# RWKV-7 inverse in 32x32 diagonal blocks, with VectorE's transpose in place of a second product chain

## The chip, the cores and the metric
The kernel runs on one core of one Trainium2 chip. The metric is the device time of one execution in microseconds (us); lower is better. Before the change it is 1394.63 us, the median of three runs (1394.05 to 1394.86).

## The reference
Two transformer-like blocks follow each other on 256 tokens of width 1024. The change touches one part of the second: the RWKV-7 state recurrence of its first layer, for 16 heads of 64:

```python
def step(S, inp):
    r_t, w_t, k_t, v_t, a_t, b_t = inp
    sa = jnp.einsum('bhvk,bhk->bhv', S, a_t)
    S = S * w_t[:, :, None, :] + sa[..., None] * b_t[:, :, None, :] + v_t[..., None] * k_t[:, :, None, :]
    y = jnp.einsum('bhvk,bhk->bhv', S, r_t)
    return S, y
```

The kernel computes it in chunks of 128 tokens. Within a chunk `sa` depends on itself through a strictly lower triangular matrix A, so the vectors u of a chunk solve (I - A) u = rhs, and the kernel needs the inverse of I - A on diagonal blocks of 64.

## The kernel before
Everything outside `Rwkv`'s core is dense products of split fp32 weights (lines 291 to 293) and is not touched. The core runs 8 units: 2 chunks of 128 tokens times 4 groups of 4 heads. Two units overlap: unit u-1 is in its second half while unit u is in its first, and the two use separate PSUM banks, so one trip of the loop (a *round*) holds the first half of one unit and the second half of the one before. There is no scheduler: the order of every engine is the order in which `pe_core`, `act_core` and `dve_core` list the steps, and semaphores hold a step until its data are there.

The steps of a unit:
- *columns* (L2722): 8 transposes by TensorE, copied out by ScalarE.
- *pairs* (L2739): 8 products of 256 columns, then VectorE multiplies each of the 4 results by a mask (L3011).
- *a_mat* (L2753): A the other way round, from which VectorE starts X (L3020); Y, X's transpose, is started from the masked pairs (L3028).
- *levels* 0 to 4: block size 1, 2, 4, 8, 16 doubles to 32, and in level 5 of 6 (n = 4) to 64. Each level is *z* (L2767, A times X), a copy by ScalarE (L2947), then *xy*: X is updated by Y and Z (L2782) and Y by Z and Y (L2786), each joined under a mask by VectorE (L3035 for X, L3042 for Y). The last level makes Y only.
- *rhs* (L2797, L2800), *u_first* (L2810), *carry* (L2818, L3050), *u_second* (L2826): the solution on the first and the second 64 tokens.
- *state* (L2836, L2837, L3060; first chunk only) and *y* (L2845 to L2851, L2961).

All of it works on 64 x 64 tiles of the array. The first and second half of the tokens sit crossed (rows of one half, columns of the other), made so by the `crossed` matrix in *columns*. A product in fp32 shows in the trace as two weight loads and two matmuls, so a *z* of 8 products is 16 matmuls there.

Of the kernel before, what the change touches and what calls it, by code (L numbers as in the profile page):

```python
# [21 lines left out]
U8 = mybir.dt.uint8  # L22
# [46 lines left out]
for _n, _w in (("ident", 128), ("cos", 64), ("sin", 64), ("causal", 384), ("invalid", 384), ("dist", 384), ("tri", 129),  # L69
               ("ends", 2), ("upper", 512), ("pair", 128), ("ident64", 64), ("crossed", 128)):  # L70
    CONSTS[_n] = (_at, _w)
    _at += _w
N_CONST = _at
LEVELS = 5
HALF = P // 2
COLUMN_TILES = (slice(0, HALF), slice(HALF, P))


def shape_constants():
# [10 lines left out]
    put("crossed", np.roll(eye, HALF, 1))  # L90
# [16 lines left out]
    turned = np.roll(strict, HALF, 1)  # L107
    put("upper", np.stack([turned, full, turned, full], 1).astype(np.float32))
    put("pair", (s // HALF == t // HALF).astype(np.float32))
    r, q = (i % HALF)[:, None], np.arange(HALF)[None, :]  # L110
    put("ident64", (r == q).astype(np.float32))
    lev = np.zeros((P, 2, LEVELS + 1, HALF), np.float32)
    for n in range(LEVELS + 1):
        b = 2 ** n
        same = r // (2 * b) == q // (2 * b)
        lev[:, 0, n], lev[:, 1, n] = same & (r // b < q // b), same & (r // b > q // b)
# [60 lines left out]
def build(nc, a, out):  # L177
    with ExitStack() as ctx:
# [25 lines left out]
        levels = sb("levels", [P, 2, LEVELS + 1, HALF], U8)  # L204
# [879 lines left out]
        class SetUp:  # L1084
# [22 lines left out]
            def sp_rest(self, sp):  # L1107

                sp.dma_start(consts[:, P:N_CONST], a["consts"][:, P:N_CONST]).then_inc(levels_loaded, 16)
                sp.dma_start(levels[:, :, :, :].rearrange("p a l s -> p (a l s)"), a["levels"]).then_inc(levels_loaded, 16)  # L1110
# [1033 lines left out]
        class TimeMix:  # L2144
# [13 lines left out]
            def __init__(self):  # L2158
# [17 lines left out]
                self.identity, self.first_x, self.first_y = sem(n + "identity"), sem(n + "first_x"), sem(n + "first_y")  # L2176
                self.z, self.z_done = [sem(f"{n}z{x}") for x in range(2)], [sem(f"{n}z_done{x}") for x in range(2)]
                self.x, self.x_done = [sem(f"{n}x{x}") for x in range(2)], [sem(f"{n}x_done{x}") for x in range(2)]
                self.inv_y, self.inv_y_done = [sem(f"{n}inv_y{x}") for x in range(2)], [sem(f"{n}inv_y_done{x}") for x in range(2)]
# [33 lines left out]
                self.x_inv = [by_head(flat(3, 0, 256)), by_head(front[:, 0:256])]  # L2213
                self.y_inv = [by_head(flat(3, 256, 256)), by_head(front[:, 256:512])]
                self.z_buf = [by_head(gain_b[1][:, 512:768]), by_head(front[:, 512:768])]
# [477 lines left out]
            def crossed(self):  # L2693

                first, second = slice(0, HALF), slice(HALF, P)
                return (first, second), (second, first)

# [12 lines left out]
            def pe_columns(self, T, u):  # L2710
# [9 lines left out]
                for j in range(2):  # L2720
                    for n, slot in enumerate((7, 4, 2, 5)):
                        mm = T.e.transpose(self.stream_banks(s)[2 + j][:, n * P:(n + 1) * P], self.pair_rows(slot, t, g, j),  # L2722
                                           const("crossed") if n == 0 else ident)
                    mm.then_inc(*T.one(self.turned))

            def pe_pairs(self, T, u):
# [3 lines left out]
                T.e.wait_ge(self.cols, 2 * (u + 1))  # L2730
                if i:
                    T.e.wait_ge(self.state_done, min(u - 1, self.GROUPS))
                for j in range(2):
                    if i and j:
                        T.e.wait_ge(self.y_done, u - 1)
                    for a in range(2):
                        for e in range(2):
                            part = slice(e * HD, (e + 1) * HD)
                            mm = T.e.matmul(self.stream_banks(s)[2 * j + e][:, 256 * a:256 * a + 256], fm[part, j, 2 + a, :],  # L2739
                                            fm[part, j, 0:2, :].rearrange("p a s -> p (a s)"), start=True, stop=True)  # L2740
                            if a:
                                mm.then_inc(*T.one(self.pairs))

            def pe_a_mat(self, T, u):
# [4 lines left out]
                for j in range(2):  # L2749
                    for at, there in self.crossed():  # L2750
                        for e in range(2):
                            part = slice(e * HD, (e + 1) * HD)
                            mm = T.e.matmul(acc[at, s, e * 512 + j * HALF:e * 512 + (j + 1) * HALF], fm[part, j, 0, there], fm[part, j, 2, at],  # L2753
# [3 lines left out]
            def pe_z(self, T, u, n):  # L2757

                s, i, t, g = self.place(u)
                if n == 0:  # L2760
                    T.e.wait_ge(self.masked, 4 * u + 4)
                    T.e.wait_ge(self.first_x, 2 * (u + 1))
                else:
                    T.e.wait_ge(self.x_done[s], (LEVELS - 1) * i + n)
                for m in range(4):
                    for at, there in self.crossed():
# [3 lines left out]
            def pe_xy(self, T, u, n):  # L2770

                s, i, t, g = self.place(u)
                if n == 0:
                    T.e.wait_ge(self.first_y, 2 * (u + 1))
                else:
                    T.e.wait_ge(self.inv_y_done[s], LEVELS * i + n)
                T.e.wait_ge(self.z_done[s], LEVELS * i + n + 1)
                for m in range(4):
                    at_m = slice(m * HALF, (m + 1) * HALF)
                    if n < LEVELS - 1:  # L2780
                        for at, there in self.crossed():
                            mm = T.e.matmul(acc[at, s, 512:1024][:, at_m], self.y_inv[s][there, m, :], self.z_buf[s][there, m, :], start=True, stop=True)  # L2782
                        if m == 3:
# [1128 lines left out]
```

## Time and profile before

| | |
|---|---|
| time, median of 3 runs | 1394.63 us |
| profiled execution: span from the first to the last instruction | 1392.2 us |
| TensorE busy | 1362.8 us (98%) |
| VectorE, ScalarE busy | 855.2 us (61%), 696.6 us (50%) |
| RWKV core, from its first columns to the last unit's y | about 778 to 916 us of the span |
| one round of the core | 14.35 us |

Of the profiled execution itself only the span is given; the median of the runs lies 2.4 us above it. A busy TensorE in this profile is not TensorE at its peak: each matmul counts from its start to its modelled end, about 0.22 us for the small ones, while the next ones have started; so the rows that follow are read by the starts. In a merged row "811.48 0.69 ... x16" the first of 16 instructions starts at 811.48 and the last ends 0.69 us later.

### The profile page before, as it was taken

Reading aid. Unit: us, or ns where it says so; the run is one execution under the profiler, and the core shown is the slowest. Engines: PE = TensorE matmul, PEld = TensorE weight load, DVE = VectorE, ACT = ScalarE, POOL = GpSimd, SP = SyncE. Lnnn points to the kernel's source line nnn. Section 1 sums busy time; section 2 is a strip of 40 time slices with the busy share of each in tenths; the row PEclk is TensorE's granted clock in tenths of the full one; section 3 lists DMA queues with packets and bytes.
Section 4 is the critical chain, followed back from the end, with each engine's and each line's share of the span. In section 5 each row is a group of like instructions: output and inputs, shape, how many; then the busy total and the mean of one; then the engine's idle time right before and its main releaser. Section 6 shows DMA issues by size and latency. Waiting matters only on the chain.

```text
span 1392.2 us, 23783 instructions
## 1 busy us (share of the span) xinstructions
PE 1362.8 (98%) x8927; PEld 1117.8 (80%) x8927; DVE 855.2 (61%) x1234; ACT 696.6 (50%) x1110; POOL 38.1 (3%) x42
## 2 busy tenths in 40 slices
PE   8999999999999999999999999999999999999998
PEld 7888877778888878888787688778888887788887
DVE  4545577875755464445784788766555677555554
ACT  5444456675465464444554444235444566644442
POOL 0000000000000000000001000110000010000000
PEclk9999999999999999999999999999999999999999
DMA  8655545556444565555352101314555651265552
GB/s 294 214 181 181 181 140 202 167 188 200 161 163 157 148 207 197 189 195 186 115 196 77 61 4 33 112 46 166 181 189 184 227 175 52 83 212 194 182 184 104
DMA packets 145537, 220.25 MB, mean 158 GB/s; under 512 B 16761, under 2 KB 65295, under 8 KB 145329
## 3 DMA queue, kind: packets, MB, share of 16 engines
q1 hardware_dynamic: 145456, 219.14, 47.8%
q8 instruction: 56, 0.92, 0.3%
q14 instruction: 25, 0.20, 0.0%
HBM read 218.04 MB, written 1.05 MB: 157 GB/s over the span
## 4 chain that ended last, share of the span: by engine, by line
PE 88%; DVE 6%; ACT 3%; issue 1%; POOL 1%; DMA 1%; SPq 0%; DVEq 0%; ACTq 0%; POOLq 0%
PE acc L291 12%; PE acc L293 12%; PE gp L291 12%; PE acc L292 12%; PE gp L293 12%; PE gp L292 12%; PE tp L944 1%; PE gp L2767 1%; PE acc L2782 1%; DVE sb_w_lo L280 1%; PE acc L1280 1%; PE tp L291 1%; ACT sb_w_hi L264 1%; ACT sb_arena L407 1%; DMA sb_raw<-in_ffn_w 1%
## 5 line engine op out<-in xcount | busy, mean ns | idle before, releaser
L280 DVE TENSOR_TENSOR sb_w_lo<-sb_raw,sb_w_hi 128x1024 fp32r<-128x1024 f32 (+1 forms) x380 | 451.5, 1214 | 207.4 <-ACT sb_w_hi L264 205.7
L264 ACT ACTIVATE sb_w_hi<-sb_raw 128x1024 fp32r<-128x1024 f32 (+1 forms) x380 | 387.9, 1052 | 210.9 <-PE acc L293 106.9
L291 PE MATMUL gp<-sb_w_hi,sb_xa_hi 128*128 128x512 f32 (+1 forms) x752 | 298.5, 397 | 5.0 <-DVE sb_w_lo L280 3.5
L293 PE MATMUL gp<-sb_w_lo,sb_xa_hi 128*128 128x512 f32 (+1 forms) x752 | 291.7, 388 | 0.0
L292 PE MATMUL gp<-sb_w_hi,sb_xa_lo 128*128 128x512 f32 (+1 forms) x752 | 291.2, 387 | 0.0
L291 PEld LDWEIGHTS gp<-sb_w_hi,sb_xa_hi 128*128 128x128 f32 x752 | 141.3, 188 | 37.8 <-DVE sb_w_lo L280 6.7
L293 PEld LDWEIGHTS gp<-sb_w_lo,sb_xa_hi 128*128 128x128 f32 x752 | 141.2, 188 | 29.6
L292 PEld LDWEIGHTS gp<-sb_w_hi,sb_xa_lo 128*128 128x128 f32 x752 | 141.5, 188 | 27.1 <-issue 0.5
L291 PE MATMUL acc<-sb_w_hi,sb_mid_hi 128*128 128x512 f32 x400 | 156.2, 390 | 0.0
L293 PE MATMUL acc<-sb_w_lo,sb_mid_hi 128*128 128x512 f32 x400 | 155.8, 390 | 0.0
L292 PE MATMUL acc<-sb_w_hi,sb_mid_lo 128*128 128x512 f32 x400 | 155.7, 389 | 0.0
L809 DVE SCALAR_TENSOR_TENSOR sb_arena<-gp,sb_stat,sb_arena 128x256 f32<-128x256 f32 x44 | 19.6, 480 | 132.9 <-ACT sb_arena L786 132.9
L291 PE MATMUL acc<-sb_w_hi,sb_xa_hi 128*128 128x512 f32 (+1 forms) x240 | 94.9, 395 | 1.5 <-DVE sb_xa_lo L492 1.5
L786 ACT ACTIVATE sb_arena<-gp,sb_stat 128x256 f32<-128x256 f32 x44 | 18.9, 470 | 148.4 <-PE gp L293 148.4
L293 PE MATMUL acc<-sb_w_lo,sb_xa_hi 128*128 128x512 f32 (+1 forms) x240 | 91.9, 383 | 0.0
L292 PE MATMUL acc<-sb_w_hi,sb_xa_lo 128*128 128x512 f32 (+1 forms) x240 | 91.8, 382 | 0.0
L293 PEld LDWEIGHTS acc<-sb_w_lo,sb_mid_hi 128*128 128x128 f32 x400 | 75.1, 188 | 15.7
L292 PEld LDWEIGHTS acc<-sb_w_hi,sb_mid_lo 128*128 128x128 f32 x400 | 75.1, 188 | 15.4
L291 PEld LDWEIGHTS acc<-sb_w_hi,sb_mid_hi 128*128 128x128 f32 x400 | 75.1, 188 | 15.4
L291 PEld LDWEIGHTS acc<-sb_w_hi,sb_xa_hi 128*128 128x128 f32 x240 | 45.1, 188 | 12.0 <-issue 3.4
L293 PEld LDWEIGHTS acc<-sb_w_lo,sb_xa_hi 128*128 128x128 f32 x240 | 45.1, 188 | 9.0
L291 PE MATMUL acc<-sb_w_hi,sb_xb_hi 128*128 128x512 f32 x128 | 51.7, 404 | 0.6 <-DVE sb_xb_lo L3699 0.5
(417 smaller groups left out, 1756.8 us busy)
## 6 DMA issues: line engine op xcount, KB each, us to landing
sb_raw<-in_ffn_w SPq DMA_DIRECT2D x264, 256.0 KB, 4.3
sb_raw<-in_mlp_w SPq DMA_DIRECT2D x256, 256.0 KB, 2.9
sb_raw<-in_w_in SPq DMA_DIRECT2D x72, 256.0 KB, 3.2
sb_raw<-in_a_w_rkv SPq DMA_DIRECT2D x48, 256.0 KB, 4.1
sb_raw<-in_xattn_w_kv SPq DMA_DIRECT2D x32, 256.0 KB, 3.6
sb_raw<-in_w_out SPq DMA_DIRECT2D x16, 256.0 KB, 3.2
sb_raw<-in_xattn_w_q SPq DMA_DIRECT2D x16, 256.0 KB, 3.1
sb_raw<-in_xattn_w_o SPq DMA_DIRECT2D x16, 256.0 KB, 3.1
```

The lines of the kernel that those rows point to most:

```text
L264: A.e.activation(w_hi[:, s, :, 0:n], raw[:, r, :, 0:n], ACT.Copy).then_inc(hi_done, 1)
L280: V.e.tensor_tensor(w_lo[:, s, :, 0:n], raw[:, r, :, 0:n], w_hi[:, s, :, 0:n].bitcast(F32), ALU.subtract).then_inc(lo_done, 1)
L291: e.matmul(dst, xh, wh, start=start, stop=False)
L292: e.matmul(dst, xl, wh, start=False, stop=False)
L293: return e.matmul(dst, xh, wl, start=False, stop=stop)
L407: A.e.activation(junk, src(t), ACT.Square, accum_out=self.st[:, t:t + 1]).then_inc(*A.one(self.squared))
L786: A.e.activation(self.silu[:, t, 0:256], gp[:, t, 0:256], ACT.Silu, scale=self.norm.st[:, t:t + 1]).then_inc(self.acted, 1)
L809: V.e.scalar_tensor_tensor(self.mid_rows[:, t, 0:256], gp[:, t, 256:512], self.norm.st[:, t:t + 1], self.silu[:, t, 0:256], ALU.mult, ALU. ...
L944: mm = T.e.transpose(tp[:, b, (2 * j + t) * P:(2 * j + t + 1) * P], self.mid_rows[:, t, at:at + P], ident)
L1280: mm = T.e.matmul(self.side(n)[:, j * self.KEYS[t]:(j + 1) * self.KEYS[t]], q, kk, start=True, stop=True)
L2767: mm = T.e.matmul(gp[there, s, m * HALF:(m + 1) * HALF], self.mt[s][at, m, 0, there], self.x_inv[s][at, m, :], start=True, stop=True)
L2782: mm = T.e.matmul(acc[at, s, 512:1024][:, at_m], self.y_inv[s][there, m, :], self.z_buf[s][there, m, :], start=True, stop=True)
```

## The change
- X, Y and Z now live in 32 x 32 diagonal blocks, four per 128 tokens. Levels 0 to 3 run on four 32 x 32 tiles: *z* has 16 products instead of 8, *x* 16.
- Y is no longer made by products: after each masked update of X, VectorE transposes it block by block (`flip`). The products of L2786 are gone.
- Level 4 becomes *join*: *z* with 8 products from the even to the odd blocks, then 16 products that put the off-diagonal block and the turned odd block of X beside each other; ScalarE writes the even block with a scale of 1 or 0 per partition and the joined part into the 64-wide `y_wide`.
- The halves are no longer crossed.
- *pairs* is cut in two, *state* is cut from *y*, and all three orders are written anew.

TensorE's queue, the round of u = 2 from the end of the previous *y* to *rhs*. Before (L2739 pairs, L2767 z of unit 1, level 3, L2800 rhs, L2753 a_mat, L2782 and L2786 xy of unit 1):

```order
L2739 MATMUL acc<-sb_shade 128x256 x4
L2739 MATMUL gp<-sb_shade 128x256
L2739 MATMUL tp<-sb_shade 128x256
L2739 MATMUL gp<-sb_shade 128x256
L2739 MATMUL tp<-sb_shade 128x256
L2767 MATMUL gp<-sb_shadow,sb_shade 64x64 x8
L2800 MATMUL tp<-sb_arena,sb_shade 64x64 x8
L2753 MATMUL acc<-sb_shade 64x64 x8
L2782 MATMUL acc<-sb_shadow 64x64 x2
```

and after (L2765 z, L2735 pairs, L2782 x, L2768 the z of level 4, L2808 rhs, L2793 and L2794 join):

```order
L2765 MATMUL gp<-sb_shadow,sb_shade 32x32 x16
L2735 MATMUL acc<-sb_shade 128x256 x4
L2782 MATMUL acc<-sb_shadow 32x32 x16
L2735 MATMUL gp<-sb_shade 128x256
L2735 MATMUL tp<-sb_shade 128x256
L2735 MATMUL gp<-sb_shade 128x256
L2735 MATMUL tp<-sb_shade 128x256
L2768 MATMUL gp<-sb_shadow,sb_shade 32x32 x8
L2808 MATMUL tp<-sb_arena,sb_shade 64x64 x8
L2793 MATMUL acc<-sb_shadow 32x32
L2794 MATMUL acc<-sb_consts,sb_shadow 32x32
```

The old unit's levels 3 and 4 have moved into and around the pairs of the new one, and the a_mat of the new one behind them.

TensorE's queue, the same round from the carry of unit 1 on. Before (L2818 carry, L2767 z of level 2, L2722 columns, L2826 u_second, L2782 xy):

```order
L2818 MATMUL acc<-sb_arena,sb_shade 64x64 x4
L2767 MATMUL gp<-sb_arena 64x64 x8
L2722 MATMUL gp<-sb_consts,sb_arena 128x128 x4
L2722 MATMUL tp<-sb_consts,sb_arena 128x128 x4
L2826 MATMUL acc<-sb_arena,sb_shadow 64x64 x4
L2782 MATMUL acc<-sb_gain_b,sb_arena 64x64 x2
```

and after, from u_first on (L2818 u_first, L2765 z of levels 0, 1, 2, L2719 columns, L2782 x of levels 0 and 1, L2826 carry, L2834 u_second, L2844 state):

```order
L2818 MATMUL acc<-sb_arena,sb_shadow 64x64 x4
L2765 MATMUL gp<-sb_arena 32x32 x16
L2719 MATMUL gp<-sb_consts,sb_arena 128x128 x4
L2719 MATMUL tp<-sb_consts,sb_arena 128x128 x4
L2782 MATMUL acc<-sb_gain_b,sb_arena 32x32 x16
L2826 MATMUL acc<-sb_arena,sb_shade 64x64 x4
L2765 MATMUL gp<-sb_arena 32x32 x16
L2834 MATMUL acc<-sb_arena,sb_shadow 64x64 x4
L2782 MATMUL acc<-sb_gain_b,sb_arena 32x32 x16
L2765 MATMUL gp<-sb_arena 32x32 x16
L2844 MATMUL acc<-sb_arena 128x128
```

The columns now stand between z and x of level 0, and almost every step is followed by one with another tile size.

VectorE's queue, the round of u = 2. Before (L3011 masks, L3020 first X, L3035 X and L3042 Y, L3028 first Y):

```order
L3011 TENSOR_TENSOR sb_shade<-acc,sb_consts 128x512 x2
L3011 TENSOR_TENSOR sb_shade<-gp,sb_consts 128x512
L3011 TENSOR_TENSOR sb_shade<-tp,sb_consts 128x512
L3020 COPY_PREDICATED sb_shadow<-sb_levels,acc 128x2x64 x2
L3035 COPY_PREDICATED sb_arena<-sb_levels,acc 128x256
L3028 COPY_PREDICATED sb_shadow<-sb_levels,sb_shade 64x256 x2
L3042 COPY_PREDICATED sb_arena<-sb_levels,acc 128x256
L3035 COPY_PREDICATED sb_shadow<-sb_levels,acc 128x256
L3042 COPY_PREDICATED sb_arena<-sb_levels,acc 128x256
```

and after (L3041 masks, L3064 X, L3073 and L3055 transposes, L3050 first X; L280 is a piece of weight splitting that is not part of the core):

```order
L3041 TENSOR_TENSOR sb_shade<-acc,sb_consts 128x512
L3064 COPY_PREDICATED sb_arena<-sb_levels,acc 128x128
L3041 TENSOR_TENSOR sb_shade<-acc,sb_consts 128x512
L3073 STREAM_TRANSPOSE sb_arena<-sb_arena 128x128
L3041 TENSOR_TENSOR sb_shade<-gp,sb_consts 128x512
L3041 TENSOR_TENSOR sb_shade<-tp,sb_consts 128x512
L3050 COPY_PREDICATED sb_shadow<-sb_levels,acc 128x2x2x32
L3055 STREAM_TRANSPOSE sb_shadow<-sb_shadow 128x128
L280 TENSOR_TENSOR sb_w_lo<-sb_raw,sb_w_hi 128x1024 x2
L3064 COPY_PREDICATED sb_shadow<-sb_levels,acc 128x128
```

The old unit's level 3 is handled between the masks, and the foreign work of 2 instructions of 128x1024 (here L280, in other rounds other ones) stands before the X of level 0; it stood before the X of level 2.

The diff, cut to its core:

```diff
             def pe_z(self, T, u, n):
...
                 for m in range(4):
-                    for at, there in self.crossed():
-                        mm = T.e.matmul(gp[there, s, m * HALF:(m + 1) * HALF], self.mt[s][at, m, 0, there], self.x_inv[s][at, m, :], start=True, stop=True)
+                    dst = gp[:, s, m * BLOCK:(m + 1) * BLOCK]
+                    if n < LEVELS - 1:
+                        for at in BLOCKS:
+                            mm = T.e.matmul(dst[at], self.mt[s][at, m, 0, at], self.x_inv[s][at, m, :], start=True, stop=True)
+                    else:
+                        for even, odd in (BLOCKS[0:2], BLOCKS[2:4]):
+                            mm = T.e.matmul(dst[odd], self.mt[s][even, m, 0, odd], self.x_inv[s][even, m, :], start=True, stop=True)
                 mm.then_inc(*T.one(self.z[s]))
...
+            def pe_x(self, T, u, n):
...
+                T.e.wait_ge(self.z_done[s], LEVELS * i + n + 1)
+                for m in range(4):
+                    dst = acc[:, s, 512 + m * BLOCK:512 + (m + 1) * BLOCK]
+                    for at in BLOCKS:
+                        mm = T.e.matmul(dst[at], self.y_inv[s][at, m, :], self.z_buf[s][at, m, :], start=True, stop=True)
+                mm.then_inc(*T.one(self.x[s]))
+
+            def pe_join(self, T, u):
+
+                s, i, t, g = self.place(u)
+                T.e.wait_ge(self.inv_y_done[s], (LEVELS - 1) * (i + 1))
+                T.e.wait_ge(self.z_done[s], LEVELS * (i + 1))
+                for m in range(4):
+                    dst = acc[:, s, 512 + m * BLOCK:512 + (m + 1) * BLOCK]
+                    for even, odd in (BLOCKS[0:2], BLOCKS[2:4]):
+                        T.e.matmul(dst[even], self.z_buf[s][odd, m, :], self.y_inv[s][odd, m, :], start=True, stop=True)
+                        mm = T.e.matmul(dst[odd], self.x_inv[s][odd, m, :], const("ident32")[odd], start=True, stop=True)
+                mm.then_inc(*T.one(self.joined))
...
                 for u in range(1, self.UNITS):
-                    self.pe_pairs(T, u)
                     self.pe_z(T, u - 1, 3)
+                    self.pe_pairs(T, u, 0)
+                    self.pe_x(T, u - 1, 3)
+                    self.pe_pairs(T, u, 1)
+                    self.pe_z(T, u - 1, 4)
                     self.pe_rhs(T, u - 1)
+                    self.pe_join(T, u - 1)
                     self.pe_a_mat(T, u)
...
+            def act_join_even(self, A, u):
+
+                s, i = u % 2, u // 2
+                A.e.wait_ge(self.inv_y_done[s], (LEVELS - 1) * (i + 1))
+                A.e.activation(self.y_wide[s][:, :, 0:BLOCK], self.y_inv[s], ACT.Copy, scale=const("even")).then_inc(*A.one(self.joined_done))
...
+            def flip(self, V, s):
+
+                V.e.wait_ge(*V.last)
+                return V.e.transpose(self.y_inv[s].rearrange("p m d -> p (m d)"), self.x_inv[s].rearrange("p m d -> p (m d)"))
```

## Rows read from the trace of the kernel before

**Rows 1.** The page: busy time by engine, and TensorE's clock in 40 slices
```profile
PE 1362.8 (98%) x8927; PEld 1117.8 (80%) x8927; DVE 855.2 (61%) x1234; ACT 696.6 (50%) x1110; POOL 38.1 (3%) x42
PEclk9999999999999999999999999999999999999999
```
**Rows 2.** Windows by stage (span; busy us of PE, PEld, DVE, ACT, POOL; clock; DMA)
```profile
778.40:794.60 16.20, 14.44 (x218) 11.04 (x218) 7.88 (x15) 5.29 (x14) 0.00 (x0) 1.00 0.00 2
808.90:823.30 14.40, 13.72 (x350) 11.93 (x346) 12.08 (x24) 7.15 (x15) 0.00 (x0) 1.00 0.02 4
```
**Rows 3.** Timeline of TensorE, first part of a round (start, us, instruction)
```profile
810.87 0.68 PE L2767 MATMUL gp<-sb_shadow,sb_shade 64*64 64x64 f32 x16
811.48 0.69 PE L2800 MATMUL tp<-sb_arena,sb_shade 128*64 128x64 f32 x16
812.09 0.46 PE L2753 MATMUL acc<-sb_shade 64*64 64x64 f32 x16
812.37 0.22 PE L2786 MATMUL acc<-sb_shadow 64*64 64x64 f32 x1
812.38 0.22 PE L2782 MATMUL acc<-sb_shadow 64*64 64x64 f32 x2
812.39 0.26 PE L2786 MATMUL acc<-sb_shadow 64*64 64x64 f32 x2
812.80 0.22 PE L2786 MATMUL acc<-sb_shadow 64*64 64x64 f32 x1
813.33 0.68 PE L2767 MATMUL gp<-sb_arena 64*64 64x64 f32 x16 [0.31 <-DVE sb_arena L3020]
```
**Rows 4.** Timeline of TensorE, the rest of that round
```profile
813.82 0.66 PE L2767 MATMUL gp<-sb_shadow,sb_shade 64*64 64x64 f32 x16
814.58 0.27 PE L2782 MATMUL acc<-sb_gain_b,sb_arena 64*64 64x64 f32 x2
...
815.11 0.63 PE L2786 MATMUL acc<-sb_shadow 64*64 64x64 f32 x16
815.79 0.68 PE L2767 MATMUL gp<-sb_arena 64*64 64x64 f32 x16
816.32 0.65 PE L2810 MATMUL acc<-sb_arena,sb_shadow 64*64 64x64 f32 x8
817.05 0.27 PE L2782 MATMUL acc<-sb_gain_b,sb_arena 64*64 64x64 f32 x2
...
817.59 0.63 PE L2818 MATMUL acc<-sb_arena,sb_shade 64*64 64x64 f32 x8
818.26 0.68 PE L2767 MATMUL gp<-sb_arena 64*64 64x64 f32 x16
```
**Rows 5.** Timeline of VectorE and ScalarE, same round
```profile
812.89 0.29 DVE L3020 COPY_PREDICATED sb_arena<-sb_levels,acc 128x128 f32<-128x128 uint8 x1
813.56 0.92 DVE L3028 COPY_PREDICATED sb_arena<-sb_levels,sb_arena 64x256 f32<-64x256 uint8 x2
815.30 0.44 DVE L3035 COPY_PREDICATED sb_arena<-sb_levels,acc 128x256 f32<-128x256 uint8 x1 [0.35 <-PE acc L2782]
816.52 0.38 ACT L2947 ACTIVATE sb_gain_b<-gp 128x256 f32<-128x256 f32 x1 [1.62 <-PE gp L2767]
```
**Rows 6.** Timeline of TensorE and ScalarE elsewhere: wide weights, a 512-wide copy
```profile
755.77 1.06 PE L2511 MATMUL tp<-sb_consts,sb_arena 128*128 128x1 f32 x9
833.92 0.60 ACT L2933 ACTIVATE sb_arena<-gp 128x512 f32<-128x512 f32 x1 [0.19 <-PE gp L2722]
```
**Rows 7.** Timeline of TensorE, start of the core
```profile
786.38 0.68 PE L2767 MATMUL gp<-sb_arena 64*64 64x64 f32 x16
794.59 0.49 PE L2739 MATMUL acc<-sb_arena 64*128 64x256 f32 x2
```
**Rows 8.** Timeline of VectorE: foreign work in a round; the end of the core
```profile
833.27 2.34 DVE L280 TENSOR_TENSOR sb_w_lo<-sb_raw,sb_w_hi 128x1024 fp32r<-128x1024 f32 x2
901.27 0.69 DVE L3255 TENSOR_TENSOR sb_arena<-sb_arena,tp 128x512 f32<-128x512 f32 x1 [0.55 <-PE tp L2867]
```

More of the change, by code:

```diff
@@ L74 @@
 LEVELS = 5
+BLOCK = 32
 HALF = P // 2
 COLUMN_TILES = (slice(0, HALF), slice(HALF, P))
+BLOCKS = tuple(slice(at, at + BLOCK) for at in range(0, P, BLOCK))
 def shape_constants():
@@ L2778, in pe_xy @@
                 for m in range(4):
[L2779 to L2783, printed above, removed]
-                            mm.then_inc(*T.one(self.x[s]))
-                    for at, there in self.crossed():
-                        mm = T.e.matmul(acc[there, s, 0:512][:, at_m], self.z_buf[s][there, m, :], self.y_inv[s][there, m, :], start=True, stop=True)
@@ L2872, in pe_core @@
                 self.pe_v_token(T, 1, range(0, 1))
-                self.pe_pairs(T, 0)
+                for j in range(2):
+                    self.pe_pairs(T, 0, j)
                 self.pe_v_token(T, 1, range(1, 2))
@@ L2963, in act_core @@
             def act_core(self, A):
-                self.act_columns(A, 0)
+                for j in range(2):
+                    self.act_columns(A, 0, j)
                 self.act_identity(A, 0)
@@ L2968, in act_core @@
                 self.act_z(A, 0, 1)
-                self.act_columns(A, 1)
+                for j in range(2):
+                    self.act_columns(A, 1, j)
                 self.act_z(A, 0, 2)
@@ L2994, in act_core @@
                 self.act_z(A, last, 4)
+                self.act_join_even(A, last)
                 self.act_gn(A, 1)
-                for g in range(2):
-                    self.turn.act_wide(A, 0, g, self.spare_bank(g), XA)
+                self.turn.act_wide(A, 0, 0, self.spare_bank(0), XA)
+                self.act_join(A, last)
+                self.turn.act_wide(A, 0, 1, self.spare_bank(1), XA)
                 self.act_rhs(A, last)
@@ L3001, in act_core, with dve_mask @@
                 self.act_y(A, last)
-            def four(self, mask):
-                return mask.unsqueeze(1).to_broadcast([P, 4, HALF])
-            def dve_masks(self, V, u):
+            def dve_mask(self, V, u, m):
                 s = u % 2
-                for m in range(4):
-                    V.e.wait_ge(self.pairs, 4 * u + m + 1)
-                    V.e.tensor_tensor(self.mt[s][:, m].rearrange("p a s -> p (a s)"), self.stream_banks(s)[m], const("upper"), ALU.mult).then_inc(*V.one(self.masked))
+                V.e.wait_ge(self.pairs, 4 * u + m + 1)
+                V.e.tensor_tensor(self.mt[s][:, m].rearrange("p a s -> p (a s)"), self.stream_banks(s)[m], const("upper"), ALU.mult).then_inc(*V.one(self.masked))
@@ L3013, in dve_first_x @@
             def dve_first_x(self, V, u):
                 s = u % 2
-                V.e.wait_ge(self.identity, 2 * (u + 1))
+                V.e.wait_ge(self.identity, u + 1)
                 V.e.wait_ge(self.a_mat, u + 1)
-                for e in range(2):
-                    src = acc[:, s, e * 512:e * 512 + 2 * HALF].rearrange("p (j d) -> p j d", j=2)
-                    V.e.copy_predicated(self.x_inv[s][:, e::2, :], levels[:, 1, 0, :].unsqueeze(1).to_broadcast([P, 2, HALF]), src).then_inc(*V.one(self.first_x))
@@ L3022, in dve_first_y @@
-            def dve_first_y(self, V, u):
-                s = u % 2
-                V.e.wait_ge(self.identity, 2 * (u + 1))
-                V.e.wait_ge(self.masked, 4 * u + 4)
-                for at, there in self.crossed():
-                    V.e.copy_predicated(self.y_inv[s][there], levels[at, 0, 0, :].unsqueeze(1).to_broadcast([HALF, 4, HALF]),
-                                        self.mt[s][at, :, 0, there]).then_inc(*V.one(self.first_y))
+                src = acc[:, s, :].rearrange("p (e n) -> p e n", e=2)[:, :, 0:2 * BLOCK].rearrange("p e (j d) -> p e j d", j=2)
@@ L3127, in dve_core @@
                 self.dve_x(V, last, 3)
-                self.dve_y(V, last, 3)
+                self.dve_y(V, last)
                 for b in range(2):
@@ L3132, in dve_core @@
                 self.dve_gn_centre(V, 1)
-                self.dve_y(V, last, 4)
                 for g in range(2):
```

214 lines of the change are left out of this document (110 added, 104 removed).

## Prediction
> **What bounds the kernel now.** I read the page first, then the windows, then the core's timeline, one engine after the other. On the page TensorE is busy 98% of the span and its granted clock is 1.00 (2.4 GHz) in every slice [rows 1]. For the core that 98% says little, so go to a round: of 14.4 us VectorE is busy 12.1, ScalarE 7.2, and TensorE "13.7" [rows 2], but each small matmul counts 0.22 us from start to modelled end. What matters is the starts. In a *z* row the 16 starts fill 0.68 - 0.22 = 0.46 us; then look at the gap from the last start of a step to the first of the next:
> - z of level 0 to z of level 4: 813.33 + 0.46 = 813.79, next 813.82: 0.03. This is the price of a step without a wait, at the same tile size [rows 3, 4].
> - z to rhs: 811.33 to 811.48, 0.15. rhs to a_mat: 811.95 to 812.09, 0.14. The tile size changes (64*64, 128*64, 64*64) and each change costs about 0.12 more [rows 3].
> - Larger ones are waits. Into z of level 0: 812.80 to 813.33, 0.50 net of the 0.03. Into x of level 0: 814.26 to 814.58, 0.29. z of level 1: 815.52 to 815.79, 0.24. x of level 1: 816.75 to 817.05, 0.27. z of level 2: 818.00 to 818.26, 0.23 [rows 3, 4]. Together 1.5 us a round.
>
> The waits are the chain of one level, 813.33 to 815.79 = 2.46 us: z 0.46 of starts and 0.22 to the end, 0.05, ScalarE's copy 0.38 [rows 5], 0.14 back, x 0.47 and 0.22, 0.03, VectorE's 0.44 [rows 5], 0.05. So a round is about 12.8 us of TensorE issuing, tile changes included, and 1.5 of waiting on short links: both must be counted.
>
> **How long a 32x32 step takes.** Before has no 32x32 product, so it is bounded by rows. u_first (L2810) is on one tile: (0.65 - 0.22)/7 = 0.061 per instruction. z is on two tiles: 0.46/15 = 0.031. a_mat is on four: (0.46 - 0.22)/15 = 0.016 [rows 3, 4]. So each tile takes an instruction every 0.06 us and the tiles run side by side; five instructions start within 0.02 us (812.37 to 812.39) [rows 3], so no general issue limit of 0.016 exists. Width: with weights of 128 columns and a single moving column it is (1.06 - 0.25)/8 = 0.10 [rows 6]; 64 columns give 0.06. In proportion 32 columns give 0.031; a straight line through both points gives 0.042; not falling at all gives 0.061. I take 0.031 (nearest to proportional use, since 128 to 64 nearly halves it). A 32x32 z, x or join is 8 instructions on each tile: 0.25 us. Ends: 0.25 and 0.48.
>
> **TensorE, per round.**
> - z of levels 0 to 4: 5 x (0.46 - 0.25) = 1.05 less (level 4 has two tiles with 8 each, the same 0.25).
> - xy of levels 0 to 3: 0.47 to 0.25, 4 x 0.22 = 0.9 less. The last xy (0.41) against join (0.25): 0.15 less. a_mat: 32 instructions on 8 tiles instead of 16 on 4, no change. Sum -2.1.
> - Tile size changes: before 8 a round (pairs, z, rhs, a_mat, columns, u_second, state, y). After 19: by the new order only x of level 1 and z of level 2 follow each other at one size. 11 x 0.12 = +1.3, and +0.1 because pairs, which starts slowly, is entered twice.
> - Net -0.7 of issuing.
>
> The Trainium skill, "TensorEngine Tiling (Array Packing)", Key Properties, says "Mode switching requires drain"; the 0.15 against 0.03 above agrees. It is the rule that speaks against this order. The same page, Instruction Overhead, gives each matmul about 60 cycles whatever its width, which would be 0.025 us at 2.4 GHz and leaves a proportional 0.031 just possible on one tile; were it paid by every instruction one after the other, a 32x32 step would be 32 x 0.025 = 0.8, which the five starts in 0.02 us contradict.
>
> **The short links.** ScalarE's copy of 128 columns: 256 take 0.38, 512 take 0.60 [rows 5, 6], so 128 take about 0.28. VectorE's masked copy of 128x128 is 0.29 (L3020) against 0.44 [rows 5]. The transpose is in no row: from 0.20 to 0.46 (half of the 0.92 of the two SBUF copies L3028) [rows 5]; I take 0.30, next to the masked copy of its size. A level's chain falls from 2.46 to 0.25 + 0.22 + 0.05 + 0.28 + 0.14 + 0.25 + 0.22 + 0.03 + 0.29 + 0.05 = 1.78. Y isn't on it: X is done, the transpose adds 0.35, and x of the next level needs it only after z and its copy (0.94). VectorE's load falls by about 2.5 of 12.1 a round: first X 0.29, first Y 0.6, X 4 x 0.15, Y 2.2 to 1.2.
>
> But the new order puts less between the links. Waits after, with what stands between:
> - z of level 0: its masks and first X (4.4 us from pairs on before, 0.50 of it waited) are covered by x3, z4, rhs, join, a_mat and u_first. None.
> - z of level 1 behind carry: x, 0.25 + 0.29 + 0.05 = 0.6, carry with its change 0.6. Up to 0.2, since the foreign 2.34 us on VectorE [rows 8] now stands before that copy, against about 2.3 us of u_first, z, columns and x.
> - u_second: VectorE does X, the transpose and then the add of the carry; about 0.3 behind z of level 1.
> - z of level 2 straight behind x of level 1: 0.6, nothing between.
> - x of level 3 behind half the pairs (1.0 us): y's copy, the identity and a 1.05 us split stand before it on ScalarE in rounds 1 to 3, 0.6 there, else none; 0.3 on average. Others 0.2.
> Sum 1.6, as before (1.5). Round: 14.35 - 0.7 + 0.1 = 13.75.
>
> **Sum.** Six rounds at -0.6: -3.6. The last (no columns to cover z of level 0) -0.1. Start of the core, z of level 0 at 786.38 to the next pairs at 794.59, 8.2 us [rows 7]: three z and three x shorter by about 0.2 each, and five of the links between (0.1 to 0.15 each) uncovered there: -1.7. Then z of level 3 comes first and waits for X: +0.4. End: VectorE waits for a gate product behind x of level 3 [rows 8], which comes 0.4 earlier; the later solution steps lie between dense products and give nothing. Total -5.4; less 0.4 for the transposes' self-waits on VectorE that reach the carry: -5.0. The span goes from 1392.2 to 1387.2 and the time, 2.4 above it, from 1394.6 to 1389.6.
>
> **The rivals.**
> - *A. Transitions are dearer.* Each change costs 0.2 instead of 0.12 because four tiles of short products must be emptied before a wide one: 19 changes x 0.08 = +1.5 a round, half of it in time that would be waited: +0.7, 7 rounds +5: 1394.5, no change. For: into pairs and columns the first gap is visibly longer. Against: 0.12 is measured three times. A transpose of 0.46 instead of 0.30 lands nearby (+0.3 a round, 1391.7). Together 0.22.
> - *B. Narrow tiles save nothing (slower).* The interval on a tile stays 0.06. The nine 32x32 steps of before's levels and join then take 0.48 each: +0.23 x 10 = +2.3 a round, of which 0.9 falls in the waits at z of level 2 and u_second: +1.4, x 7 = +10, and +1 at the start: 1400.6. It turns slower than before from 0.045 us per instruction on a tile. For: it is paid by twice the number of products. Against: 0.10 at 128 columns and 0.06 at 64. 0.15.
> - *C. The links matter more than the issue.* If the changes cost no more than 0.06 between 64*64 and 32*32 (only the row count might matter), 0.5 a round more is won: 1386. 0.10.
> - The clock: with shorter bursts TensorE could fall to 1.2 GHz in the core. At 1.00 throughout, also in the start with more idle time [rows 1, 2], it has 0.02.
>
> **Numbers.** Forecast 1389.6, chance 0.51, own range 1387 to 1392.5. No change is within 0.2%, 2.8 us, about what a measurement of this kernel can tell. Faster by more: nearly all of the forecast's range and C, 0.59. Same: A and the forecast's upper edge, 0.23. Slower: B, the dear end of A, the clock, 0.18. The range that holds 8 of 10 runs from 1385.5 (C) to 1398 (B at 0.055).
>
> **What would show it.** Right: a 32x32 row x32 of about 0.47 from first start to last end; gaps of 0.12 to 0.15 between steps of unequal tiles; rounds of 13.7; STREAM_TRANSPOSE near 0.30; VectorE under 10 us a round; the largest wait before z of level 2. Wrong: x32 rows of 0.7; gaps of 0.2 and more; rounds above 14.3; x of level 0 waiting behind the foreign VectorE work; a clock under 1.00 between 778 and 916 us.

## The result

The changed kernel takes 1409.8 us (median of 4 runs, 1404.5 to 1410.6), the kernel before 1394.7 us beside it: ratio 1.0098, 95% interval [1.0087, 1.0110]. It is slower by about 15 us; 1389.6 was forecast and the range ended at 1398. The profiled execution took 1404.5 us with a span of 1402.7, 10.5 more than before's 1392.2.

The page of the changed kernel, against [rows 1] (the last row is the queue that brings instructions: packets, MB, share):

```profile
PE 1364.0 (97%) x9695; PEld 1114.3 (79%) x9695; DVE 839.3 (60%) x1210; ACT 691.9 (49%) x1118; POOL 38.1 (3%) x42
PEclk9999999999999999999999998799999999999999
q8 instruction: 62, 1.02, 0.3%
```

TensorE has 768 matmul instructions more and as many weight loads, and two slices of its clock row are clearly below full speed; in before's row none is. Next the six rounds of the core, from one pairs step to the next (span; busy of PE, PEld, DVE, ACT, POOL; clock; DMA share; GB/s). First one round of before (its other five: 14.13 to 14.35; all six 85.85), then the changed kernel:

```profile
808.94:823.28 14.34, 13.66 (x348) 11.90 (x344) 12.02 (x24) 7.15 (x15) 0.00 (x0) 1.00 0.02 4
```
```profile
793.39:808.57 15.18, 13.85 (x451) 11.51 (x441) 8.88 (x20) 5.28 (x14) 0.00 (x0) 0.89 0.01 3
808.57:822.70 14.13, 12.22 (x449) 10.07 (x440) 9.81 (x21) 6.41 (x17) 0.00 (x0) 1.00 0.02 5
822.70:836.73 14.03, 12.50 (x450) 10.19 (x440) 10.04 (x21) 6.60 (x18) 0.00 (x0) 1.00 0.02 4
836.73:852.86 16.13, 14.06 (x444) 11.64 (x441) 9.69 (x21) 5.44 (x15) 0.00 (x0) 0.89 0.02 4
852.86:870.43 17.57, 15.07 (x457) 12.79 (x448) 11.31 (x21) 4.85 (x16) 0.00 (x0) 0.76 0.19 62
870.43:888.20 17.77, 14.76 (x455) 12.17 (x448) 9.28 (x19) 5.60 (x16) 3.80 (x1) 0.79 0.02 4
```

The second and third round are 0.2 to 0.3 us shorter than before's. The other four are longer, and in each of them the granted clock is under 1.00: part of the round ran at 1.2 GHz and the rest at 2.4. The steps themselves are as forecast. TensorE in the second round (start, us, instruction), answering to [rows 3, 4]:

```profile
812.96 0.37 PE L2749 MATMUL acc<-sb_shade 64*32 64x32 f32 x32
813.44 0.68 PE L2818 MATMUL acc<-sb_arena,sb_shadow 64*64 64x64 f32 x8
814.04 0.45 PE L2765 MATMUL gp<-sb_arena 32*32 32x32 f32 x32
815.45 0.45 PE L2782 MATMUL acc<-sb_gain_b,sb_arena 32*32 32x32 f32 x32
815.84 0.68 PE L2826 MATMUL acc<-sb_arena,sb_shade 64*64 64x64 f32 x8
817.09 0.45 PE L2765 MATMUL gp<-sb_arena 32*32 32x32 f32 x32 [0.58 <-DVE sb_arena L3064]
817.89 0.68 PE L2834 MATMUL acc<-sb_arena,sb_shadow 64*64 64x64 f32 x8 [0.35 <-DVE sb_arena L3080]
```

A row of 32 lasts 0.45 us, less the 0.19 of its last one 0.26 of starts (forecast 0.25). From the last start of z (814.04 + 0.26) to the first transpose of *columns* (814.43) is 0.13, from the last start of x (815.71) to carry 0.13: the gap at a tile size change is 0.12 to 0.15 as in [rows 3]. VectorE's new rows, against [rows 5]:

```profile
813.90 0.31 DVE L3055 STREAM_TRANSPOSE sb_arena<-sb_arena 128x128 f32<-128x128 f32 x1
816.75 0.29 DVE L3064 COPY_PREDICATED sb_arena<-sb_levels,acc 128x128 f32<-128x128 uint8 x1
```

So the cause is in none of these prices. What is new is a pause in the middle of a step, here in z of level 0 in the fifth round, which waits for no engine:

```profile
858.25 0.45 PE L2765 MATMUL gp<-sb_shadow,sb_shade 32*32 32x32 f32 x30
860.19 0.21 PE L2765 MATMUL gp<-sb_shadow,sb_shade 32*32 32x32 f32 x2 [1.49 <-issue]
860.34 0.66 PE L2719 MATMUL gp<-sb_consts,sb_arena 128*128 128x128 f32 x4
```

Thirty matmuls have been issued and the last two come 1.5 us late; "issue" says that nothing in the profile held them. The waits of TensorE from 780 to 925 us (us in total, times, longest) have these, 6.6 us in all, where before has a single one of 0.6 us:

```profile
PE gp L2765 <- issue: 5.1, 6, 1.8
PE tp L2857 <- issue: 1.0, 1, 1.0
PE acc L2749 <- issue: 0.5, 1, 0.5
```

The trace's DMA records show a packet of 16,384 bytes on the instruction queue starting at 857.94, and the pause ends 2.25 us later. The page's count of these packets grows with TensorE's instructions: 56 in before, 62 here, that is 6 for 1,536 more instructions (matmuls and weight loads), 256 to a packet. The same holds in every trace: the fourteen of this case have 65 such pauses between 780 and 925 us, and each ends 2.2 to 3.0 us after a packet's start.

The clock fell before any pause: the first round has a clock of 0.89 and no pause, and the first pause in the core ends at 828.93, in the third round. Behind the sixth round the clock is low again:

```profile
900.00:910.00 10.00, 7.69 (x173) 5.38 (x169) 2.24 (x5) 0.94 (x3) 0.00 (x0) 0.69 0.05 14
```

### The profile page after: what moved, and what is told of

Same layout as the page of the kernel before. It is cut to its first block, busy times and chain, and to the rows that moved or that the text cites. A ratio compares the mean times of both kernels' runs of the same rounds, so it can differ in the third digit from the quotient of the medians.

```text
span 1402.7 us, 25295 instructions
## 1 busy us (share of the span) xinstructions
PE 1364.0 (97%) x9695; PEld 1114.3 (79%) x9695; DVE 839.3 (60%) x1210; ACT 691.9 (49%) x1118; POOL 38.1 (3%) x42
## 4 chain that ended last, share of the span: by engine, by line
PE 88%; DVE 5%; ACT 4%; issue 1%; DMA 0%; POOL 0%; SPq 0%; DVEq 0%; ACTq 0%; POOLq 0%
PE acc L291 12%; PE acc L293 12%; PE acc L292 12%; PE gp L291 12%; PE gp L293 12%; PE gp L292 12%; PE tp L944 1%; DVE sb_w_lo L280 1%; PE acc L2782 1%; ACT sb_w_hi L264 1%; PE gp L2765 1%; ACT sb_arena L407 1%; PE gp L2735 1%; PE acc L1280 1%; PE tp L291 1%
## 5 line engine op out<-in xcount | busy, mean ns | idle before, releaser
L280 DVE TENSOR_TENSOR sb_w_lo<-sb_raw,sb_w_hi 128x1024 fp32r<-128x1024 f32 (+1 forms) x380 | 451.6, 1214 | 206.0 <-ACT sb_w_hi L264 204.5
L293 PEld LDWEIGHTS acc<-sb_w_lo,sb_mid_hi 128*128 128x128 f32 x400 | 75.1, 188 | 15.6
```

The costliest lines, as they stand in the source:

```text
L280: V.e.tensor_tensor(w_lo[:, s, :, 0:n], raw[:, r, :, 0:n], w_hi[:, s, :, 0:n].bitcast(F32), ALU.subtract).then_inc(lo_done, 1)
L293: return e.matmul(dst, xh, wl, start=False, stop=stop)
```

## The experiments

Two theories at first. T: instructions come too late for dense rows of small products, and the clock falls behind these pauses. O: the new order leaves TensorE waiting, and the clock falls by that (called I, for idle time, in the expectations of the halved kernel). Times are medians with the ratio to before.

### The two halves of the change apart

**Order alone**: before's products, all three engines in the new order of steps.

```diff
-                    self.pe_pairs(T, u)
                     self.pe_z(T, u - 1, 3)
+                    self.pe_pairs(T, u, 0)
+                    self.pe_xy(T, u - 1, 3)
+                    self.pe_pairs(T, u, 1)
+                    self.pe_z(T, u - 1, 4)
```

> The products of before (64x64 tiles, Y by products, crossed halves) issued in the new order of steps on all three engines. Theory O (the new order is what costs: it leaves TensorE waiting with nothing between, and its clock is then granted lower in the core): 1403 to 1412 us, granted clock under 1.00 in several stretches between 790 and 910 us, few pauses inside a step. Theory T (the many 32x32 products cost: instructions arrive late and TensorE pauses inside a step): 1394 to 1398 us, clock 1.00 in the core, at most one pause of over 0.3 us inside a step, since the number of instructions is that of before.

1413.7 us, 1.0135 [1.0113, 1.0157]. The time is near O's, the reason mostly is not. Rounds three and four of six, and the longest waits of the six:

```profile
830.36:846.97 16.61, 14.25 (x348) 12.07 (x345) 11.62 (x24) 6.92 (x16) 0.00 (x0) 1.00 0.01 2
846.97:864.99 18.02, 15.66 (x347) 13.33 (x344) 11.48 (x24) 5.97 (x15) 0.00 (x0) 0.91 0.01 3
```
```profile
PE gp L2767 <- DVE sb_arena L3045: 4.4, 6, 1.0
PE gp L2767 <- DVE sb_shadow L3045: 4.1, 6, 1.0
PE acc L2782 <- ACT sb_shadow L2954: 2.8, 4, 0.7
```

At a clock of 1.00 a round lasts 16.6 us: the order puts too little between the links of a level, and 64-wide links (0.38 and 0.44 us of copying) are longer than 32-wide ones (0.28 and 0.29). The order fits only the narrow blocks.

**32x32 tiles in before's order**: the new products, transposes and join; only the order of steps is before's.

```diff
-                    self.pe_pairs(T, u, 1)
+                    self.pe_z(T, u, 0)
                     self.pe_z(T, u - 1, 4)
-                    self.pe_rhs(T, u - 1)
+                    self.pe_x(T, u, 0)
                     self.pe_join(T, u - 1)
...
```

> The new arithmetic (32x32 tiles, join, transposes on VectorE) in before's order of steps. Theory O: 1388 to 1392 us, clock 1.00 in the core. Theory T: 1404 to 1412 us, five or more pauses of 0.3 to 2 us inside 32x32 steps (each ending 2 to 3 us after an instruction fetch began), and a granted clock under 1.00 after them.

1423.2 us, 1.0208 [1.0191, 1.0225]: slower still, and beyond T's 1404 to 1412, with 12.0 us of pauses in all and a clock of 0.67 to 0.80 in every round. TensorE waits for the other engines less here than in before (3.9 us against 4.8 from 780 to 925), so the low clock can't be put down to such waits. Here z, z of level 4, x, join and z stand back to back. One round, and the longest pause, while weights are also being loaded:

```profile
828.53:847.05 18.52, 16.85 (x445) 14.51 (x441) 10.35 (x21) 6.87 (x16) 0.00 (x0) 0.67 0.01 3
```
```profile
905.14 0.44 PE L2782 MATMUL acc<-sb_shadow 32*32 32x32 f32 x29
909.00 0.32 PE L2782 MATMUL acc<-sb_shadow 32*32 32x32 f32 x3 [3.41 <-issue]
```

So neither half is innocent, and the new order is the better one for narrow tiles.

**Transpose alone**: 64x64 tiles and before's order; Y of levels 0 to 3 by VectorE's transpose, halves no longer crossed.

```diff
-                    for at, there in self.crossed():
-                        mm = T.e.matmul(acc[there, s, 0:512][:, at_m], self.z_buf[s][there, m, :], self.y_inv[s][there, m, :], start=True, stop=True)
...
+                if n < LEVELS - 1:
+                    self.flip(V, s).then_inc(*V.one(self.inv_y_done[s]))
```

> Only the transpose goes to VectorE: 64x64 tiles and before's order stay, levels 0 to 3 of Y are transposes of X in 32-wide blocks, the last level of Y stays a product. TensorE has 32 matmul instructions fewer a round (xy 0.47 to 0.24 us, four times). If pauses come from instruction supply (T): none here, 0.9 us a round less issuing, of which half shows up as longer waits: 1388 to 1392 us, clock 1.00. If the clock falls wherever TensorE waits more than 1.5 us of a 14 us round (idleness theory): 1396 to 1405 us, clock under 1.00 in the core without a pause inside a step.

1394.1 us, 0.9995 [0.9986, 1.0005]: no change (1388 to 1392 was expected), one pause of 0.5 us where before has one of 0.6, clock 1.00. The saving wasn't there to be had: half the products issue in nearly the same time.

```profile
811.50 0.65 PE L2780 MATMUL acc<-sb_shadow 64*64 64x64 f32 x16
```

0.65 - 0.22 is 0.43 us of starts for 16, where before's xy took 0.47 for 32: X and Y ran side by side on four tiles, and X alone uses two.

### Is it the supply of instructions?

**Dummies in one row**: before, with 96 products of 32x32 (384 instructions; their results are not used) behind the pairs of each of the seven rounds. **Dummies spread**: the same 96 in six rows of 16.

```diff
+                for k in range(n):
+                    at = slice(32 * (k % 4), 32 * (k % 4) + 32)
+                    T.e.matmul(tp[at, s, 256:288], ident[at, at], ident[at, at], start=True, stop=True)
```

> Before with 96 products of 32x32 (identity by identity, results unused) in one row between pairs and z of level 3 in each of the seven rounds: 384 instructions, with weight loads, that TensorE could issue in 1.5 us, plus one tile change each way. If instructions come as fast as TensorE can issue: 1.5 to 1.8 us a round, 1404 to 1408 us. If their supply is limited (T): pauses of 1 us and more inside the row in nearly every round, row length 2.5 to 4 us, 1411 to 1422 us.

> Before with the same 96 products of 32x32 in six rows of 16 behind the z and xy steps of a round. TensorE's own issue costs as much as in one row (0.12 to 0.15 us a row) and each row brings two tile changes (0.25 us): 1.5 + 1.5 = up to 3 us a round, less about 1 us that falls into waits. If supply matters only in dense stretches (T): few pauses, 1408 to 1412 us. If it is the number of instructions per round that matters: as many and as long pauses as in the one row, 1418 us or more. Clock 1.00, because less of the round is idle than in before; under 1.00 if narrow products themselves let it fall.

One row: 1424.6 us, 1.0213 [1.0196, 1.0230]; spread: 1426.5 us, 1.0243 [1.0216, 1.0269]. First the one row, then one of the spread ones:

```profile
851.59 1.65 PE L2873 MATMUL tp<-sb_consts 32*32 32x32 f32 x173
855.59 0.37 PE L2873 MATMUL tp<-sb_consts 32*32 32x32 f32 x19 [2.34 <-issue]
```
```profile
875.52 0.26 PE L2873 MATMUL tp<-sb_consts 32*32 32x32 f32 x6
876.62 0.41 PE L2873 MATMUL tp<-sb_consts 32*32 32x32 f32 x26 [0.83 <-issue]
```

Pauses appear in a kernel that had one: 15.6 us (9 of them) and 12.0 us (14). The one row is above the 1411 to 1422 us expected for T; the spread ones are far above T's 1408 to 1412 and fit the 1418 or more expected if the number of instructions counts. In four of seven rounds the one row itself issued in 1.63 to 1.7 us, and the pauses came in steps behind it; spreading helps little. It is the number of instructions in a round that counts, not the dense stretch alone. And the second half of T falls, at least in the rounds: with these pauses the clock stays at 1.00 in all six rounds of the spread kernel. Only behind them, around a pause of 2.4 us that ends at 914.70, is it low. One round, then that stretch:

```profile
867.08:885.24 18.16, 15.99 (x548) 13.96 (x544) 10.94 (x23) 5.26 (x13) 0.00 (x0) 1.00 0.23 61
910.00:920.00 10.00, 7.42 (x257) 6.38 (x256) 2.60 (x7) 1.15 (x3) 0.00 (x0) 0.69 0.69 259
```

**Half the products**: the changed kernel with heads 0 and 1 only in z, x and join. **One product for two heads**: heads in pairs, 64 moving columns behind one head's weights, so that heads 1 and 3 are multiplied by those of heads 0 and 2.

```diff
                         for at in BLOCKS:
-                            mm = T.e.matmul(dst[at], self.mt[s][at, m, 0, at], self.x_inv[s][at, m, :], start=True, stop=True)
+                            mm = T.e.matmul(dst[at], self.mt[s][at, m, 0, at], self.x_inv[s][at, m:m + 2, :].rearrange("p m d -> p (m d)"), start=True, stop=True)
...
```

> The changed kernel with only two of the four heads in every z, x and join step, so half of its small products are left out; order, waits and the other engines' work stay. Theory T (late instructions come first, and the clock falls behind the pauses): no pause of over 0.3 us inside a 32x32 step, granted clock 1.00 in the core, and a round of 13.0 to 13.7 us, since each step issues in half the time but most of that was next to a wait: 1384 to 1391 us. Theory I (TensorE works too little in the core: short narrow steps between waits let its clock fall by themselves): no pauses, but a clock at or below the 0.98 mean of the changed kernel, 1400 us or more.

> The changed kernel with one product for two heads in every z, x and join step: the weights of head 0 (or 2) and 64 moving columns, so half the products, each twice as wide; heads 1 and 3 are computed with the wrong weights. Instructions as in the kernel with half the products (8 a step on each pair of passes), tiles still 32x32. If late instructions cost the 7 us of pauses in the changed kernel: none of over 0.3 us inside a 32x32 step except behind a data transfer. If the narrow tiles between waits lower the clock by themselves: granted clock under 1.00 in the core all the same, 1391 to 1400 us. If the clock falls through the number of instructions or the pauses: 1.00 in the core and 1386 to 1391 us. The step lasts 0.13 us where the interval on a tile is set by the weights, 0.25 us where it is set by the moving columns.

1393.5 us, 1.0003 [0.9986, 1.0019], and 1397.7 us, 1.0026 [1.0012, 1.0040]; the first is in neither of the ranges expected for it. No pause within a small step in either; the paired kernel has none in the whole core (the halved one has 1.7 us in *columns*, behind the loads of gn_g and gn_b). With the dummies this shows both ways that the pauses come with the number of instructions. But both kernels lose clock without them. The paired one:

```profile
793.64:809.47 15.83, 14.28 (x294) 11.27 (x288) 9.77 (x20) 5.41 (x15) 0.00 (x0) 0.81 0.01 2
824.72:838.30 13.58, 11.94 (x295) 9.28 (x288) 9.40 (x21) 6.37 (x17) 0.00 (x0) 1.00 0.01 3
```

13.58 us at 1.00 is what the changed round would be with instructions always there and steps of 0.21 instead of 0.26 us; ten steps at 0.05 make it 14.08, and 14.03 and 14.13 were measured. Of its ten timed runs the fastest had a mean clock of 0.995 and took 1392.5, the slowest 0.985 and 1403.0: 1.1 us for each thousandth, and a line through the ten ends near 1387 at 1.00. That is extrapolated, no run shows it. It also says how to read what follows: the clock of one and the same kernel differs by up to 0.010 from one execution to the next, so the rounds of a single traced execution tell little of a small difference.

**Shifted blocks**: 32 small products ahead of the core, half a packet of instructions.

> The changed kernel with 32 products of 32x32 more (128 instructions with weight loads, half a fetch of 256) some 100 us ahead of the core, about 0.5 us of issue. If the pauses come where a block of 256 instructions is late: they move to other steps of the core (by about half a block, some 2 us), and the sum stays between 4 and 9 us; time within 3 us of the changed kernel's. If they belong to steps or waits of the schedule: the same steps pause at the same places by the same amounts.

1408.0 us, 1.0103 [1.0086, 1.0120]. The pauses move, 5.3 us in all (6.6 in the changed kernel), as expected if they come where a packet is late; the longest is now in a_mat, which had 0.5:

```profile
856.00 0.26 PE L2752 MATMUL acc<-sb_arena 64*32 64x32 f32 x7
857.70 0.33 PE L2752 MATMUL acc<-sb_arena 64*32 64x32 f32 x25 [1.44 <-issue]
```

**Small group-norm loads**: gn_g and gn_b cut to 32 columns.

```diff
-                sp.dma_start(self.gn_gain, a["a_gn_g_2"][0].partition_broadcast(P))...
+                sp.dma_start(self.gn_gain[:, 0:32], a["a_gn_g_2"][0][0:32].partition_broadcast(P))...
```

> The changed kernel with the two 512 KB loads of gn_g and gn_b cut to 32 of their 1024 columns (the rest of both stays unloaded). In the changed kernel the longest pause of the middle rounds (1.71 us) ends behind an instruction fetch that began as the last packet of these loads was out. If the fetch was held up by that transfer: the fetch comes some 2 us earlier, that pause is 0 to 0.9 us, the later ones behind the weight transfers stay; the span is 1 to 3 us shorter. If pauses depend on the instruction rate alone: 1.5 us or more stays at that place, no difference.

In the changed kernel these loads run from 853.99 to 857.94, and the packets of instructions around them start at 851.70 and 857.94, 6.2 us apart. Here they start 4.3 us apart (854.70, 858.97), and the pause at the same instruction shrinks from 1.49 to 0.40 us:

```profile
860.43 0.45 PE L2765 MATMUL gp<-sb_shadow,sb_shade 32*32 32x32 f32 x30
861.27 0.21 PE L2765 MATMUL gp<-sb_shadow,sb_shade 32*32 32x32 f32 x2 [0.40 <-issue]
```

It again ends 2.3 us after the packet's start. So a data transfer can hold up instructions. Other traces agree: in the changed kernel the packet starts within 0.01 us of the loads' end, in the halved one too (858.47, pause 1.7 us), and the changed kernel's longest pause (1.8 us) follows a packet that came 6.9 us behind the one before, during weight transfers. The changed kernel's five pauses of 0.3 to 1.0 us in the rounds have packets 4.3 to 5.2 us apart and no data transfer ahead of them. The time, 1406.1 us, 1.0084 [1.0067, 1.0101], isn't told apart from the changed kernel's: other pauses took its place (6.4 us in all).

### What lets the clock fall?

**Fillers**: the changed kernel, and the one with half the products, with five 128x128 products of the identity in each round's waits.

```diff
+                    self.pe_fill(T, (u - 1) % 2, 2)
                     self.pe_x(T, u - 1, 3)
...
```

> The changed kernel with five 128x128 products of the identity in each round (two ahead of x of level 3, one each ahead of z of level 1, u_second and z of level 2), which fill TensorE's waits and whose results nobody reads. If the clock falls because of idle time alone: granted clock 1.00 in the core, pauses inside steps remain (about 5 us in all), 1394 to 1400 us. If the clock falls because of the pauses in the instruction supply: still under 1.00 behind them, 1406 to 1414 us. The fillers themselves cost at most 0.3 us a round where the wait was shorter than they are.

> The same half of the products, and the five 128x128 identity products a round in the waits. If both causes act (pauses from supply, clock from idle time), this takes both away: clock 1.00 in the core, no pause, 1388 to 1393 us. If late instructions alone matter, it is no faster than the half without fillers (0.1 to 0.3 us a round slower). If the clock alone matters, it is 10 us or more faster than that one.

1405.8 us, 1.0095 [1.0061, 1.0128], and 1397.8 us, 1.0019 [1.0002, 1.0036]. One round of each, the first and the fourth, and a stretch behind the rounds of the first kernel:

```profile
793.75:808.01 14.26, 13.98 (x459) 11.45 (x450) 8.86 (x20) 5.25 (x14) 0.00 (x0) 1.00 0.01 3
```
```profile
833.39:846.47 13.08, 12.84 (x299) 10.25 (x299) 9.65 (x21) 5.40 (x16) 0.00 (x0) 1.00 0.02 4
```
```profile
890.00:900.00 10.00, 6.87 (x186) 5.62 (x188) 5.06 (x9) 1.21 (x4) 0.00 (x0) 0.63 0.58 207
```

With fillers the clock is 1.00 in five of six rounds (0.90 in the other), against 0.89, 1.00, 1.00, 0.89, 0.76, 0.79 without; in the halved kernel 1.00 four times and then 0.83 and 0.84, against 0.70, 0.87, 0.81, 0.95, 0.77, 0.72. The timed runs bear this out for the first kernel only in part: mean clocks of 0.985 to 0.994 in four runs, against 0.983 to 0.988 in the changed one, and a time whose interval overlaps the changed kernel's. For the halved kernel they don't: its ten runs have 0.980 to 0.990 without fillers and 0.983 to 0.993 with them, and the time is no shorter. So what TensorE does in its waits plays a part in the clock; how large a part isn't shown. Behind the rounds, where no fillers stand, the clock falls with them too. And a filler changes two things at once: it ends empty time, and it is a product that uses all of the array, where a 32x32 product uses a small part of it. No run tells the two apart. My 1394 to 1400 for the first and 1388 to 1393 for the second were missed.

**Half the products of before**: 64x64 tiles, before's order, heads 0 and 1 only in z and xy.

> Before, in its own order and with its 64x64 tiles, but with only two of the four heads in every z and xy step (the rest of these products is left out). Each of the ten steps issues in half the time, the chain of a level and the work of ScalarE and VectorE stay, so TensorE waits longer than in before: about 4 us of a 14 us round, more than in the changed kernel or in the one with two heads per product. If waiting alone lets the clock fall: granted clock under 1.00 in the core from the first round on, 1396 us or more. If it takes the 32x32 tiles: 1.00 in the core and 1385 to 1393 us. No pauses inside a step in either case, since instructions are fewer than in before.

1392.6 us, 0.9982 [0.9964, 1.0000]. Three rounds at 1.00, then one at 0.70:

```profile
806.25:819.66 13.41, 11.61 (x233) 9.76 (x233) 11.85 (x24) 7.06 (x16) 0.00 (x0) 1.00 0.01 2
832.81:849.76 16.95, 15.68 (x237) 13.26 (x233) 12.60 (x24) 6.21 (x14) 0.00 (x0) 0.70 0.01 2
```

Narrow tiles aren't needed for the clock to fall; that halving the products on 64x64 tiles is enough, these runs show (mean clocks 0.987 to 0.996 in ten runs, before 0.998 to 1.000). Neither expectation holds as written: it falls, but not from the first round, and the time is under 1396.

## Why the prediction was wrong

- **Step length, tile changes, copies, transpose**: right. 0.26 us (forecast 0.25), gaps of 0.12 to 0.15 at a change (the same), VectorE's copy and transpose 0.29 and 0.31 (0.29 and 0.30). Rivals A, B and C are out.
- **Round at full clock**: 14.03 to 14.13, forecast 13.75. Issuing was well met (11.8 us, forecast 12.15), the waits were not: in the second round, net of the changes, x of level 3 0.5, u_first 0.15, z of level 1 0.66, u_second 0.4, z of level 2 0.6, in all 2.3 against 1.6. The largest miss is z of level 1, for which up to 0.2 had been put: the foreign work on VectorE reaches further into the round than I summed (until 816.8 here, when x has been done since 815.9). Six rounds of 14.08, the mean of the two, are 1.4 us less than before's six, instead of -3.6. The start of the core, pairs to pairs, went from 13.69 to 12.99: -0.7 instead of -1.3.
- **The missing term**: the forecast priced an instruction by its tile and took its supply as given ("no general issue limit"). The five starts within 0.02 us excluded a limit inside TensorE, not one of the fetch. This step failed: instructions come in packets, and where they are many in a round, or a data transfer delays a packet, TensorE stands still. In rounds four to six the pauses delay the next start by 0.67 + 0.82 + 1.68 + 0.75 + 1.1 = 5.0 us, and by some 2.6 more in the last stretch.
- **The clock**: the step that failed outright. It had a chance of 0.02, because before stays at 1.00 "also in the start with more idle time", and no term in the sum. The changed core runs at 0.89, 0.89, 0.76 and 0.79 in four of its six rounds. Against a clean round of 14.08, and without the pauses, the first, fourth, fifth and sixth round lose 1.1 + 0.6 + 1.8 + 1.8 = 5.3 us.
- The sum for the profiled execution: earlier arrival at the core -0.5, start -0.7, clean rounds -1.4, pauses +5.0, clock +5.3, last stretch +2.7: 10.4 of the 10.5 us. In the last stretch pauses and a low clock (0.69 from 900 to 910) act together, and what it would be without them isn't known. The timed runs are 5 us longer than the profiled one at like mean clocks (0.983 to 0.988); that isn't explained.

What the runs show: more instructions in a round bring the pauses and fewer take them away, by interventions both ways. What stays open is the clock. Empty time alone doesn't order the versions. From 780 to 925 us (waits for the engines and pauses) TensorE stands empty for 17.3 us in the changed kernel and has a mean clock of 0.987 over that execution; with the spread dummies it is 17.5 us at 0.996, with the order alone 19.9 us at 0.995, with 32x32 tiles in before's order 15.9 us at 0.972. The versions that keep before's X products on 64x64 tiles for all four heads are at 0.995 to 1.00 in their traces, whatever their empty time; those with 32x32 tiles or two heads only are at 0.972 to 0.993. How much of the array the products use, and not how long TensorE stands empty, is then a rival that no run here tests by itself. Why the clock falls most behind 850 us, no run settles either. No version here beats the kernel before by what can be measured.

## What to carry over

Count instructions per us, not only what each costs on its tile: splitting a product into narrow tiles doubles its instructions, and a part of the kernel that was near its supply of instructions then pauses in places no semaphore explains; look for "issue" inside a step. A tuned stretch whose TensorE clock is 1.00 may be held there by the very work that an optimisation removes (halving before's products was enough to lose it), so give the clock a price and not a chance of 0.02. Before halving products, see whether both halves already run side by side.

## What the hardware showed unexpectedly

- Each packet of instructions holds 256, takes 0.9 to 1.6 us on its queue, and a starved TensorE goes on 2.2 to 3.0 us after its start. In the cores of all fourteen traces no two of them start closer than 3.3 us; if that is the limit, which is an estimate, instructions come at best every 13 ns. A 32x32 step uses 64 (with weight loads) in 0.26 us, 4 ns each. The changed round has some 890 in 14.1 us, 16 ns each, with little left for delays. The Trainium skill, "Advanced Engine Details and Errata", section ISA Cache, names lines of 16 KB with 256 instructions; the packets agree. It also has "Only 2 cache lines", beside 128 KB on TensorE; no run shows how many TensorE has, only that 384 instructions in one row without a pause need more than one at hand.
- A row of 32x32 tiles with 64 moving columns and half the products issues in 0.21 us against 0.26.
- In the changed kernel the granted clock moved between its two levels within the core, though TensorE was never idle in its rounds for over 1.5 us at a time. The Trainium skill, "TensorE: Matmul & The Clock Gate", section "A second HAM failure mode: psum-queue depth-cycling", tells of a kernel whose short idle times between groups of matmuls made the clock go up and down. The changed kernel's trace agrees with it; those with the spread dummies and with the order alone, at 0.996 and 0.995 with as much empty time, hardly do.
